# Attention with the head values as stationary operand, the sums left with columns on partitions, and the second network's output projection mixed into its attention

## Chip, cores and metric

The kernel runs on one core of a Trainium2 chip. The metric is the device time of one execution in microseconds; the kernel before was timed three times, and the median counts. A profiled execution gives the trace; its span runs from the first instruction to the last.

## What is computed

Two networks of two layers each run one after the other on 256 tokens of width 1024, in float32. A layer of the first network has three branches (retention, a chunked attention with 8 heads of 64, and a differential attention), gates and merges them, multiplies by `w_out`, and follows with a feed-forward network. A layer of the second has a feed-forward network, then a mixer of three parts whose outputs are laid side by side (256 columns of a short convolution, 256 of a gated MLP, 512 of an attention with 8 query heads on 2 key/value heads), its output projection, and a second feed-forward network. The parts that the change touches, cut to the core:

```python
# first network, chunk attention: s are scores with a relative bias
p = jax.nn.softmax(s, axis=-1).astype(v.dtype)
o = jnp.einsum('bhqk,bkhd->bqhd', p, v)

# second network, short convolution
z = c_gate * h                       # then a causal convolution of width 3 per column: y
return b_gate * y

# second network, attention: three branches that share the queries
pc = masked_softmax(sc, cmp_end[None, :] <= t[:, None])      # 15 compressed keys
o_cmp = jnp.einsum("bgrsn,bngd->bsgrd", pc.astype(vc.dtype), vc)
...
o = g[..., 0, None] * o_cmp + g[..., 1, None] * o_s + g[..., 2, None] * o_w

mix = jnp.concatenate([y_a, y_b, y_c], axis=-1) @ w_out[l]
x = layer_norm(ALPHA * x + mix, ln2_g[l], ln2_b[l])
```

With 256 tokens the selected and the windowed branch both see all earlier keys, so each is a causal attention with keys and values of its own.

## The kernel before

A Python planner (`Plan`, `script`) writes one list of steps, and each engine's function then runs through the whole list and issues what it has to do for each step, in that order. Every engine works its own part strictly in this order and waits on semaphores for operands and free buffers.

**Weights.** A weight matrix comes in units of 1 MB (`P.unit`): SyncE loads a unit into one of three `raw` buffers, ScalarE rounds it to the high part (`high`, L1655), VectorE forms the low part (`low`, L1895), both into one of three `hl` buffers. A product of float32 precision is three rounded matmuls (`mm3`, L200 to L203: high by high, high by low, low by high), so a unit gives 48 matmuls of 256 columns or 24 of 512. Activations are kept as high and low parts too: `XT`, `O1`, `O2`, all with columns on partitions and tokens along the free axis. The step `need` that stands ahead of a unit's matmuls puts the load, the `high` and the `low` of the unit two further on into the list, in one piece.

**Attention.** The 256 queries are two blocks i = 0, 1 of 128, with K = 128(i+1) keys. A task is a block and four heads (two pairs j, each with a lower and an upper half hh of the partitions). `score_pair` (L1491) makes scores for four heads into two PSUM banks; `soft` takes the row maximum on VectorE (L2015) and the exponential on ScalarE (L1741), whose sums go to `rs`. `weigh` turns the unscaled weights in blocks of 128x128 on TensorE (L1372) and copies them to `et`, in turns by ScalarE (L1749) and VectorE (L2022). `values` (L1514) then multiplies, per head and key block, with `et` (128x128) as stationary and the head's values (128x64) as moving operand, so that queries stand on partitions:

```python
for n, (o, vs) in enumerate(outs):
    for mt, v in enumerate(vs):
        x = n * len(vs) + mt
        ins = e.matmul(o, et.ap[:, x * 128:(x + 1) * 128], v, start=mt == 0, stop=mt == len(vs) - 1)
```

In the first network `ca_norm` divides by the sums (L2045), and `turn_split` turns the result back with four transposes for each block and splits it into high and low for the projection. In the second, `nsa_collect` (L2255 to L2268) weights and adds the three branches of a block in `YC`, and `finish` turns and splits them. The compressed branch makes its values for all 8 heads (`cmp_out`, L1572, 512 columns), masks its scores (`cmp_mask`), turns them (`cmp_turn`, L1627) and multiplies (`cmp_values`, L1633). These matmuls (L1491, L1514, L1552, L1572, L1633) take float32 operands without the split, and the trace shows two matmul instructions for each of them. `cmp_hidden` (L1552) is of this kind too; its outputs lie on partitions 0 to 29 and 32 to 61 by turns, from stationary operands of 30 columns.

**Order.** `slots` runs the tasks staggered: in slot n the scores of task n, the values of n-2, the transposes of n-1. `mix(a, b, share)` lays attention steps between pieces of projection units by costs written out by hand (`PART` = 1.44 for a quarter of a unit). In the second network `SHARE2` = 1.4 mixes the attention with the last input projections; when these are used up, the attention goes on alone until all weights are turned (the mark "turned"), and what is left of it is mixed with the output projection at 0.45. The convolution (`conv`: one product, six tap steps and a last product on VectorE, then its split, L2178 to L2190 and L1809) is one step behind the last input projection. `residual` (L1453) puts the scaled input into the accumulators, `out_part` multiplies the first half of `w_out_2` (convolution and MLP rows), `out_end` the attention's half.

## Time and profile before

| what | value |
| --- | --- |
| median of 3 executions | 2088.54 us (2085.18 to 2094.77) |
| profiled execution, its own time | 2087.4 us |
| its span | 2085.4 us |
| TensorE matmul busy | 2046.5 us, 98% of the span |
| VectorE busy | 1241.1 us, 60% |
| ScalarE busy | 926.4 us, 44% |
| weights and other data read | 349.43 MB, 168 GB/s over the span |

In the profile PE is TensorE's matmul, PEld its weight load, DVE is VectorE, ACT ScalarE, POOL GpSimd, SP SyncE. A matmul's time in the trace runs from its start to its modelled end, and matmuls overlap, so the pace of a series is read from starts, and from the chain of waits, where each step is given only the time that it adds. The granted clock (PEclk) is a share of the full TensorE clock.

### The profile page before, as it was taken

What the parts mean: (1) busy time and instruction counts of PE and PEld (TensorE: products, weight loads), DVE (VectorE), ACT (ScalarE), POOL (GpSimd) and SP (SyncE); (2) the same over time, 40 slices, a digit from 0 to 9 for tenths busy, and PEclk for the clock granted to TensorE, in tenths of its full rate; (3) what the DMA queues carried; (4) which work ended last, traced back from release to release, by engine and by line L of the source; (5) the groups of instructions that cost most, each with busy time, mean ns of one, the idle gap of its engine ahead of it and who ended that gap; (6) DMA issues with size and microseconds to landing.
All of it is one profiled execution on the core that took longest, in us unless ns stands there. A gap on an engine that the chain in (4) does not pass through costs nothing.

```text
span 2085.4 us, 32609 instructions
## 1 busy us (share of the span) xinstructions
PE 2046.5 (98%) x14392; PEld 1877.9 (90%) x14392; DVE 1241.1 (60%) x1554; ACT 926.4 (44%) x1278; POOL 44.2 (2%) x56
## 2 busy tenths in 40 slices
PE   7999999999999999999999999899999999989998
PEld 6889999999888999999999988799999998879997
DVE  5555656555655565655665566565566556656555
ACT  3444544443544444444444444344444445434442
POOL 0000000000000000000000001000000000100000
PEclk9999999999999999999999999999999999999999
DMA  7544455766554455586666654258656665435663
GB/s 268 176 131 142 159 185 154 216 184 194 168 162 142 142 163 182 157 242 186 175 182 182 191 146 130 81 144 253 182 166 197 183 182 146 139 98 165 183 182 101
DMA packets 415893, 352.59 MB, mean 169 GB/s; under 512 B 28704, under 2 KB 360840, under 8 KB 415624
## 3 DMA queue, kind: packets, MB, share of 16 engines
q1 hardware_dynamic: 415752, 350.51, 56.0%
q8 instruction: 113, 1.85, 0.4%
q14 instruction: 28, 0.23, 0.0%
HBM read 349.43 MB, written 1.05 MB: 168 GB/s over the span
## 4 chain that ended last, share of the span: by engine, by line
PE 94%; DVE 3%; ACT 2%; DMA 1%; POOL 0%; issue 0%; DVEq 0%; SPq 0%
PE ps L201 28%; PE ps L202 28%; PE ps L203 28%; PE ps L1372 3%; PE ps L1514 2%; PE ps L1453 1%; PE ps L1491 1%; DVE hl L1895 1%; DMA raw<-in_w_in 1%; PE ps L1494 1%; ACT hl L1655 1%; DVE xt L1972 0%; ACT tm L1697 0%; PE ps L1552 0%; ACT er L1741 0%; PE ps L1496 0%
## 5 line engine op out<-in xcount | busy, mean ns | idle before, releaser
L1895 DVE TENSOR_TENSOR hl<-raw,hl 128x2048 fp32r<-128x2048 f32 (+2 forms) x333 | 738.6, 2222 | 466.8 <-ACT hl L1655 466.8
L201 PE MATMUL ps<-xt,hl 128*128 128x256 f32 (+1 forms) x2672 | 755.7, 283 | 0.0
L202 PE MATMUL ps<-xt,hl 128*128 128x256 f32 (+1 forms) x2672 | 746.2, 279 | 0.0
L203 PE MATMUL ps<-xt,hl 128*128 128x256 f32 (+1 forms) x2672 | 745.8, 279 | 0.0
L1655 ACT ACTIVATE hl<-raw 128x2048 fp32r<-128x2048 f32 x324 | 614.9, 1900 | 209.5 <-PE ps L203 192.1
L201 PEld LDWEIGHTS ps<-xt,hl 128*128 128x128 f32 (+1 forms) x2672 | 501.4, 188 | 4.8 <-issue 1.7
L202 PEld LDWEIGHTS ps<-xt,hl 128*128 128x128 f32 (+1 forms) x2672 | 501.2, 188 | 4.4 <-issue 1.2
L203 PEld LDWEIGHTS ps<-xt,hl 128*128 128x128 f32 (+1 forms) x2672 | 501.0, 188 | 0.2
L201 PE MATMUL ps<-hl,o 128*128 128x512 f32 x656 | 261.7, 399 | 0.0
L203 PE MATMUL ps<-hl,o 128*128 128x512 f32 x656 | 259.4, 395 | 0.0
L202 PE MATMUL ps<-hl,o 128*128 128x512 f32 x656 | 259.4, 395 | 0.0
L201 PE MATMUL ps<-hl,xt 128*128 128x512 f32 (+1 forms) x576 | 209.7, 364 | 7.2 <-DVE hl L1895 4.8
L202 PE MATMUL ps<-hl,xt 128*128 128x512 f32 (+1 forms) x576 | 202.8, 352 | 0.0
L203 PE MATMUL ps<-hl,xt 128*128 128x512 f32 (+1 forms) x576 | 202.6, 352 | 0.0
L1725 ACT ACTIVATE th<-ps 128x256 f32<-128x256 f32 x132 | 50.8, 385 | 330.9 <-PE ps L203 330.9
L203 PEld LDWEIGHTS ps<-hl,o 128*128 128x128 f32 x656 | 123.2, 188 | 29.8
L201 PEld LDWEIGHTS ps<-hl,o 128*128 128x128 f32 x656 | 123.2, 188 | 26.9 <-issue 0.5
L202 PEld LDWEIGHTS ps<-hl,o 128*128 128x128 f32 x656 | 123.3, 188 | 26.8 <-issue 0.5
L201 PEld LDWEIGHTS ps<-hl,xt 128*128 128x128 f32 x576 | 109.0, 189 | 25.6 <-DVE xt L1972 6.2
L203 PEld LDWEIGHTS ps<-hl,xt 128*128 128x128 f32 x576 | 108.8, 189 | 16.1
L202 PEld LDWEIGHTS ps<-hl,xt 128*128 128x128 f32 x576 | 109.0, 189 | 14.0
L1999 DVE SCALAR_TENSOR_TENSOR tm<-th,ps 128x256 f32<-128x256 f32 x132 | 55.5, 420 | 103.6 <-ACT th L1725 96.2
(200 smaller groups left out, 1677.3 us busy)
## 6 DMA issues: line engine op xcount, KB each, us to landing
raw<-in_w_in SPq DMA_DIRECT2D x84, 1024.0 KB, 5.1
raw<-in_w_ffn_in SPq DMA_DIRECT2D x88, 512.0 KB, 5.2
raw<-in_ffn_gate SPq DMA_DIRECT2D x88, 512.0 KB, 4.0
raw<-in_ffn_up SPq DMA_DIRECT2D x88, 512.0 KB, 5.3
raw<-in_ffn_down SPq DMA_DIRECT2D x44, 1024.0 KB, 5.1
raw<-in_w_ffn_out SPq DMA_DIRECT2D x22, 1024.0 KB, 5.3
raw<-in_w_out SPq DMA_DIRECT2D x16, 1024.0 KB, 5.1
raw<-in_w_branch_a SPq DMA_DIRECT2D x8, 1024.0 KB, 5.2
```

The source lines that it names most:

```text
L201: e.matmul(out, l[0], r[0], start=start, stop=False)
L202: e.matmul(out, l[0], r[1], start=False, stop=False)
L203: return e.matmul(out, l[1], r[0], start=False, stop=stop)
L1372: ins = e.transpose(b.ap[:, k * 128:(k + 1) * 128], x, ident)
L1453: ins = e.matmul(b.ap[:, k * 128:(k + 1) * 128], XT[:, z, 4 * c + k, i * 128:(i + 1) * 128], ai, start=first and k == 0 and z == 0, stop=n ...
L1491: e.matmul(b.ap[:, n * K:(n + 1) * K], qs[n][hh], ks[n][hh], start=n == 0, stop=False)
L1494: ins = e.matmul(b.ap[:, n * K + c:n * K + c + 128], l, r, start=False, stop=x == len(bias[hh]) - 1)
L1514: ins = e.matmul(o, et.ap[:, x * 128:(x + 1) * 128], v, start=mt == 0, stop=mt == len(vs) - 1)
L1655: e.activation(m["hl"][:, k % NHL, 0, 0:n], m["raw"][:, k % NRAW, 0:n], ACT.Copy).then_inc(s.high.up(("high", k)), 1)
L1725: e.activation(tha, ga, ACT.Tanh, scale=0.5).then_inc(done.up(th.full), 1)
L1895: e.tensor_tensor(lo[:, c], m["raw"][:, k % NRAW, 0:n][:, c], hi[:, c].bitcast(F), ALU.subtract).then_inc(s.low.up(("low", k), *([("low", ...
L1999: e.scalar_tensor_tensor(tma, tha, 1.0, ga, ALU.add, ALU.mult).then_inc(done.up(th.free), 1)
```

## The change

The constants `own` (now by key/value head) and the new `head` mask serve the compressed branch. The diff, cut:

```diff
-SHARE2 = 1.4
+SHARE2 = 0.95
...
+    def spread(self, g, piece):
+        if piece == 1:
+            self.add("need_high", g + self.ahead)
+        elif piece in (2, 3):
+            self.add("need_low", piece - 2)
...
     def n_parts(w, r, c0, src, src_events, banks, first, last, after=()):
-        g = P.unit(segs, n)
+        g = P.unit(segs, n, True)
         for i in range(2):
             for k0 in (0, 2):
                 add("n_part", ...)
+                P.spread(g, 2 * i + k0 // 2)
...
+    def out_part(w, acc, src_events, c, r=0, ks=(0, 2)):
+        segs, n = wk(w, r * 128, 4, c * 512, 512)
+        g = P.unit(segs, n, True)
+        for n, k0 in enumerate(ks):
+            for i in range(2):
...
+    def out_end(w, acc, src_events, o1_read, r=4, heads=False):
+        def rows(c):
+            if not heads:
+                return wk(w, r * 128, 4, c * 512, 512)
+            return [(lambda a, g=g: a[64 * g:64 * g + 64, 0:UNIT].rearrange("p (k c) -> p k c", k=4),
+                     w[512 + g * 256:768 + g * 256, c * 512:(c + 1) * 512].rearrange("(k p) c -> p k c", p=64)) for g in range(2)], UNIT
...
-    def slots(tasks):
+    def slots(tasks, order):
         for n in range(len(tasks) + 2):
-            for x in (n, n - 2, n - 1):
+            for x in order:          # (-1, 0, -2, -1) for these two attentions
...
+    def turned(ers, i):              # transposes and copies of weights already scaled
...
# second network's task, after score_pair
+                gate = gts[:, 24 * i:24 * i + 24].rearrange("p (g j b) -> p g j b", g=2, j=4)[:, :, 2 * jp:2 * jp + 2, bno]
+                add("scale", ers, rs, rc, (("gates", l), gate), 128 * T)
+                ets = turned(ers, i)
+                outs = [(hh, lambda ob, hh=hh: ob.ap[64 * hh:64 * hh + 64, jp * 256:(jp + 1) * 256].rearrange("p (n q) -> p n q", n=2),
+                         VS[:, mt, (bno - 1) * 128 + hh * 64:(bno - 1) * 128 + (hh + 1) * 64],
+                         ets[hh].ap[:, 0:2 * T * 128].rearrange("p (n t q) -> p n t q", n=2, t=T)[:, :, mt, :]) for mt in range(T) for hh in range(2)]
+                part(i, "values_t", ets, outs, [("v nsa", l)], [("win read", l)])
...
-        mix(chain(lin_v(), lin_q(1), lin_conv()), steps, SHARE2, False)
-        while "turned" not in at:
-            next(steps)
-        P.flush()
...
-        mix(lin_out(), steps, 0.45)
+        mix(chain(lin_v(), lin_q(1), lin_conv(), beside(chain(lin_conv2(), lin_out()), conv)), steps, SHARE2)
...
# TensorE
+    def values_t(ob, ets, outs, first, last, v_events, after):
+        for n, (hh, o, v, p) in enumerate(outs):
+            ins = e.matmul(o(ob) if callable(o) else o, v, p, start=first and n < 2, stop=last and n >= len(outs) - 2)
...
# VectorE
+    def scale(ers, rs, rc, gate, K):
+        e.reciprocal(rc, rs).then_inc(done.up(), 1)
+        if gate is not None:
+            e.tensor_tensor(r, r, gate[1], ALU.mult).then_inc(done.up(), 1)
+        for hh, er in enumerate(ers):
+            ev = er.ap[:, 0:2 * K].rearrange("p (n k) -> p n k", n=2)
+            e.tensor_tensor(ev, ev, bc(rc[:, 2 * hh:2 * hh + 2], 2, K), ALU.mult).then_inc(done.up(("scaled", er.n)), 1)
```

In words:

- The weights are divided by their sums (and multiplied by the gate) on VectorE before they are turned (`scale`). `values_t` then has the head's values, 128x64, as stationary and the turned weights as moving operand: 128 columns at a time in the first network, 256 (two heads of one key/value head) in the second. Lower and upper halves of the output partitions come by turns, first `hh` = 0, then 1. The sum stands with columns on partitions, so `ca_norm`, `nsa_collect`, `YC` and the transposes behind them go; `o_split` splits it straight from PSUM. All five sums of a block in the second network (four tasks, one compressed branch) gather in one bank.
- The compressed branch makes its values for 2 heads instead of 8 (128 columns instead of 512), scales in `cmp_mask`, spreads its turned weights by the `head` mask on VectorE, and multiplies twice by 256 columns.
- `w_out_2`'s rows of the attention are loaded in another order, as two halves of 64 partitions.
- In `n_parts`, `t_parts`, `lin_v` and `out_part` the load and `high` of a later unit now stand behind the second quarter of a unit, and `low` comes in two halves behind the third and the fourth.
- The convolution is cut into five steps that are laid beside the last input projection unit and the output projection, which itself is mixed into the attention (one `mix` at 0.95 for all).

Two places of the second network's first layer show the new order. On TensorE, the end of the attention: L1372 are the transposes of the weights `er`, L1453 the residual, L1620 the compressed scores, L1627 their transpose, L1514 the values, L201 the first matmul of each triple of the output projection (its triples go on where lines are left out). Before:

```order
L1372 MATMUL ps<-cst,er 128x128 x8
L1620 MATMUL ps<-small,q 128x15 x8
L1514 MATMUL ps<-v,et 128x64 x8
L1372 MATMUL ps<-cst,er 128x128 x8
L1453 MATMUL ps<-ai,xt 128x128 x8
L1627 MATMUL ps<-cst,er 120x128
L1514 MATMUL ps<-v,et 128x64 x8
L1453 MATMUL ps<-ai,xt 128x128 x8
L201 MATMUL ps<-hl,o 128x512
```

Now (L1408 transposes, L1489 residual, L1667 compressed scores, L1561 `values_t`, L1674 and L1683 the compressed branch, L202 to L204 the triples):

```order
L1408 MATMUL ps<-cst,er 128x128 x8
L1489 MATMUL ps<-ai,xt 128x128 x8
L202 MATMUL ps<-hl,o 128x512
...
L1667 MATMUL ps<-small,q 128x15 x8
L1561 MATMUL ps<-et,v 64x256 x4
L202 MATMUL ps<-hl,o 128x512
...
L1408 MATMUL ps<-cst,er 128x128 x8
L202 MATMUL ps<-hl,o 128x512
...
L1561 MATMUL ps<-et,v 64x256 x4
L1674 MATMUL ps<-cst,er 120x128
L1489 MATMUL ps<-ai,xt 128x128 x8
```

Two triples stand where lines are left out first, two after `values_t`, and four after the last transposes; before, no triple stood between the first row and the last.

On VectorE, the same part of the attention, with the convolution (L2178 to L2188 before, its split L1907). Before:

```order
L2015 TENSOR_REDUCE small<-ps 128x2 x2
L2178 TENSOR_TENSOR zb<-th,ps 128x2x256
L2183 TENSOR_SCALAR tm<-zb,small 128x256
L2186 SCALAR_TENSOR_TENSOR tm<-zb,small,tm 128x256 x2
L2183 TENSOR_SCALAR tm<-zb,small 128x256
L2186 SCALAR_TENSOR_TENSOR tm<-zb,small,tm 128x256 x2
L2188 TENSOR_TENSOR tm<-tm,ps 128x512
L1907 SCALAR_TENSOR_TENSOR o<-tm,o 128x512
L2022 COPY et<-ps 128x512
```

Now, from the scaling of one task (L2089 to L2098) over the next task's maximum (L2061) and one tap step of the convolution to the next scaling:

```order
L2098 TENSOR_TENSOR er<-er,small 128x512 x2
L2061 TENSOR_REDUCE small<-ps 128x2 x2
L2237 TENSOR_SCALAR tm<-zb,small 128x256
L2240 SCALAR_TENSOR_TENSOR tm<-zb,small,tm 128x256 x2
L1941 TENSOR_TENSOR hl<-raw,hl 128x1024
L1953 SCALAR_TENSOR_TENSOR o<-ps,o 128x4x128
...
L2068 COPY et<-ps 128x512
L2089 RECIPROCAL small<-small 128x4
L2094 TENSOR_TENSOR small<-small 128x4
```

The copies to `et` no longer stand behind the whole convolution, and low parts of weights come as halves between small steps; the scaling, which waits for the exponentials of its task, now stands ahead of the next task's maximum.

## Rows read from the trace of the kernel before

**Rows 1.** Busy time, share of the span and instructions of each engine (page, part 1)

```profile
PE 2046.5 (98%) x14392; PEld 1877.9 (90%) x14392; DVE 1241.1 (60%) x1554; ACT 926.4 (44%) x1278; POOL 44.2 (2%) x56
```

**Rows 2.** What TensorE waited for: us in total, times, longest

```profile
PE ps L1514 <- ACT et L1749: 7.0, 2, 3.5
PE ps L1627 <- DVE er L2246: 4.6, 2, 2.3
PE ps L1491 <- DVE o L1907: 3.2, 2, 1.6
PE ps L1491 <- ACT q L1677: 1.4, 2, 0.7
```

**Rows 3.** Busy time of each engine by stretch, then granted clock, DMA share, GB/s

```profile
1260.00:1345.00 85.00, 76.87 (x599) 69.36 (x599) 50.03 (x100) 33.22 (x92) 1.30 (x1) 0.94 0.30 95
1783.00:1868.00 85.00, 76.87 (x607) 69.78 (x606) 50.59 (x100) 33.23 (x92) 1.90 (x1) 0.96 0.32 98
130.00:230.00 100.00, 100.00 (x711) 89.38 (x710) 57.53 (x78) 45.76 (x92) 0.00 (x0) 1.00 0.44 144
```

**Rows 4.** Chain of waits, 1328 to 1337 us: start, us that the step adds

```profile
1328.37 0.70 DVE tm L2188
1329.09 0.63 ACT o L1809
1329.72 0.49 ACT et L1749
1330.26 3.68 PE ps L1514 x16
...
1336.94 1.73 PE ps L1514 x16
```

**Rows 5.** TensorE in order of time: start, us to the modelled end, line

```profile
1778.26 0.28 PE L203 MATMUL ps<-xt,hl 128*128 128x256 f32 x1
1778.46 3.69 PE L1552 MATMUL ps<-qkv,gb 128*30 128x128 f32 x64
1782.08 0.39 PE L201 MATMUL ps<-xt,hl 128*128 128x256 f32 x1
1782.30 0.28 PE L202 MATMUL ps<-xt,hl 128*128 128x256 f32 x1
```

**Rows 6.** The same view, two score groups of the first network, each between its neighbours

```profile
132.68 0.71 PE L1491 MATMUL ps<-k,q 64*128 64x128 f32 x8
133.32 0.82 PE L1494 MATMUL ps<-cst,gb 128*128 128x128 f32 x5
...
146.36 1.14 PE L1491 MATMUL ps<-k,q 64*128 64x256 f32 x8
147.42 0.71 PE L1494 MATMUL ps<-cst,gb 128*128 128x128 f32 x4
```

**Rows 7.** Groups of TensorE instructions: count, busy us, mean ns

```profile
L1514 PEld LDWEIGHTS ps<-v,et 128*128 128x128 f32 x288 | 37.7, 207 | 7.6 <-ACT et L1749 7.2
L1552 PEld LDWEIGHTS ps<-qkv,gb 128*30 128x30 f32 x128 | 6.8, 108 | 0.3
L1572 PE MATMUL ps<-w,tm 128*120 128x512 f32 x4 | 3.2, 888 | 0.0
```

**Rows 8.** Groups of VectorE and ScalarE instructions: count, busy us, mean ns

```profile
L2255 DVE RECIPROCAL small<-small 128x8 f32<-128x8 f32 x12 | 2.3, 195 | 0.0
L2268 DVE TENSOR_TENSOR sg<-sg,tm 128x512 f32<-128x512 f32 x8 | 5.5, 692 | 0.3
L2213 DVE TENSOR_TENSOR sg<-sg,gn 128x256 f32<-128x256 f32 x4 | 1.7, 425 | 0.1
L2015 DVE TENSOR_REDUCE small<-ps 128x2 f32<-128x512 f32 x32 | 20.6, 685 | 8.7 <-PE ps L1496 8.7
L1741 ACT ACTIVATE er<-ps,small 128x256 f32<-128x256 f32 x64 | 29.4, 472 | 49.9 <-DVE small L2015 49.9
L1895 DVE TENSOR_TENSOR hl<-raw,hl 128x2048 fp32r<-128x2048 f32 x313 | 716.1, 2291 | 466.8 <-ACT hl L1655 466.8
```

More of the change, by code:

```diff
@@ L311, in C, with unit @@
         return self.m["const"][:, CO[name][0]:CO[name][1]]
-    def unit(self, segs, n):
+    def unit(self, segs, n, spread=False):
         g = len(self.units)
         self.units.append((segs, n))
-        self.add("need", g + self.ahead)
-        return g
+        if not spread:
+            self.add("need", g + self.ahead)
+        return g
+    def spread(self, g, piece):
[3 more added lines that the diff above has]
+            self.add("need_low", piece - 2)
     def prep_next(self):
@@ L338, in settled @@
     def settled(self):
-        out, k, low = [], 0, {}
+        out, k, low, due = [], 0, {}, []
         def begin():
@@ L348, in settled @@
         for kind, args in self.steps:
+            if kind == "need_low":
+                for u in due:
+                    out.append(("low", (u, self.units[u][1], args[0], 2)))
+                if args[0]:
+                    due.clear()
+                continue
+            if kind == "need_high":
+                assert not due
+                while k < min(len(self.units), args[0]):
+                    due.append(begin())
+                continue
+            assert not due or kind not in ("need", "prep")
             if kind == "need":
@@ L561, in out_end @@
             P.ahead = NHL - c
-            us.append(P.unit(*wk(w, r * 128, 4, c * 512, 512)))
+            us.append(P.unit(*rows(c)))
         def part(c, i, ks):
@@ L913, in turn @@
                 TM.give(tm)
-            yield from slots([task(i, jp) for i in range(2) for jp in range(2)])
+            yield from slots([task(i, jp) for i in range(2) for jp in range(2)], (0, -2, -1))
             yield 0.5
@@ L1120, in nsa, with part @@
         def nsa():
-            rss = [(P.small(24), P.small(24)) for _ in range(2)]
-            def collect(i, bno, ob, events, first_):
-                tm = None if first_ else TM.take()
-                add("nsa_collect", l, i, bno, ob, rss[i], gts, YC[i], tm, events, first_)
-                PB.give(ob)
-                if tm:
-                    TM.give(tm)
+            obs, sums = {}, [0, 0]
+            def part(i, kind, *args):
+                if not sums[i]:
+                    obs[i] = PB.take()
+                ob = obs[i]
+                add(kind, ob, *args[:2], sums[i] == 0, sums[i] == 4, *args[2:])
+                sums[i] += 1
+                if sums[i] == 5:
+                    add("o_split", ob, range(4), (), (), [O1[:, z, 4:8, i * 128:(i + 1) * 128] for z in (0, 1)], [o1_before], [("o1 nsa", l, i)], 1.0 / ALPHA)
+                    PB.give(ob)
             def compressed(i):
-                rs, rc = rss[i]
-                er = ER.take()
-                mx = P.small(8)
+                er, mx, rs = ER.take(), P.small(8), P.small(8)
                 bs = [PB.take() for _ in range(2)]
@@ L1145, in compressed @@
                 yield 0.3
-                ob = PB.take()
-                add("cmp_values", l, ob, et)
+                part(i, "cmp_values", l, et)
                 ET.give(et)
                 yield 1.0
-                collect(i, 0, ob, [("cmp sums", l, i)], False)
-                yield 0.2
             def task(i, bno, jp):
-                rs, rc = rss[i]
-                js = (2 * jp, 2 * jp + 1)
-                hs = [[hh * 4 + j for j in js] for hh in range(2)]
+                js, T = (2 * jp, 2 * jp + 1), i + 1
+                rs, rc = P.small(4), P.small(4)
                 def K(hh, j):
@@ L1193, in nsa @@
+            main = slots([task(i, bno, jp) for jp in range(2) for i in range(2) for bno in (1, 2)], (-1, 0, -2, -1))
+            side = chain(lambda: early, at.until("q"), lambda: compressed(0), at.until("conv"), lambda: compressed(1))
             for cost in main:
@@ L1515, in values @@
         ins.then_inc(done.up(ob.full, et.free, *after), 1)
+    def values_t(ob, ets, outs, first, last, v_events, after):
+        if first:
+            e.wait_ge(*T[ob.before])
+        for et in ets:
+            e.wait_ge(*T[et.full])
+        for x in v_events:
+            e.wait_ge(*T[x])
+        for n, (hh, o, v, p) in enumerate(outs):
+            ins = e.matmul(o(ob) if callable(o) else o, v, p, start=first and n < 2, stop=last and n >= len(outs) - 2)
+        ins.then_inc(done.up(ob.full, *(et.free for et in ets), *after), 1)
     def ret_scores(l, h, b, q, k, dh, er):
@@ L2270, in vector_engine, with cmp_turn @@
-    run(steps, dict(start=start, masks=masks, low=low, turn_split=turn_split, rotate=rotate, silu_gate=silu_gate, ln_stats=ln_stats,
+        e.tensor_tensor(ev, ev, bc(rs, 2, 15), ALU.mult).then_inc(done.up(er.full), 1)
+    def cmp_turn(l, i, er, tb, et):
+        e.wait_ge(*T[tb.full])
+        e.wait_ge(*T[et.before])
+        e.tensor_tensor(et.ap[0:120, :].rearrange("p (j q) -> p j q", j=4), bc(tb.ap[0:120, 0:128], 1, 4), bc(C("head")[0:120, :], 2, 128),
+                        ALU.mult).then_inc(done.up(et.full, tb.free), 1)
```

310 lines of the change are left out of this document (149 added, 161 removed).

## The prediction

> **What bounds the kernel now.** First the page: TensorE's matmuls are busy for 98% of the span, VectorE for 60%, ScalarE for 44% [rows 1]. So whatever helps must take work or waits from TensorE, and the other two may take on work where they have room. Then the waits of TensorE [rows 2]: 7.0, 4.6, 3.2 and 1.4 us, each made of two occurrences, one for each layer of the second network. Then the stretches [rows 3]: in the two attention stages of the second network, 85 us each, matmuls are busy for 76.9 us, so 8.1 us are idle in each, and the granted clock is 0.94 and 0.96. In the first network's attention stage it is busy for all of 100 us at full clock. The chain of waits [rows 4] shows the longest wait: the convolution's last product on VectorE, its split on ScalarE (0.63), only then the copy to `et` that stood behind it in ScalarE's queue, then the values: 16 instructions in 3.68 us, where the same 16 take 1.73 a little later. The first pace is that of the half clock (1.2 of 2.4 GHz) and follows 3.5 us of idleness.
>
> **The change, part by part.**
>
> *Values.* Now 288 matmul instructions [rows 7] at 1.73/16 = 0.108 us [rows 4] make 31.1 us. The 128 columns of stationary `et` cost the same as before however few columns move. With `values_t` each product still gives two instructions, but lower and upper halves of the output partitions come by turns and may run side by side. No row shows this with 64 stationary columns. The nearest is `cmp_hidden`, whose outputs also lie in two column groups: 64 instructions take 1782.08 - 1778.46 = 3.62 us [rows 5], so 0.113 a pair for 128 moving columns. For 256 columns I add what the score groups show, four pairs in 1.06 instead of 0.64 us [rows 6], 0.105 a pair: 0.218. Going into such a group and out again costs something: from the start of L203 to that of the second plain matmul behind are 4.04 us [rows 5], less 0.24 for two plain steps and 3.62 for the pairs, 0.18. Short groups lose more: four pairs in 0.64 us are 0.19 above 4 x 0.113 [rows 6]. Between 0.18 and 0.37 I take 0.3. The first network has 48 pairs of 128 columns in 8 groups (4 pairs for a task of the first block, 8 for the second), the second network 48 pairs of 256 columns in 16 groups (2 and 4). That is 24 x 0.3 + 48 x 0.113 + 48 x 0.218 = 7.2 + 5.4 + 10.5 = 23.1 us, **8.0 less**. With 0.18 a group it is 20.2, 10.9 less.
>
> The trace's 108 ns for a load of 30 columns against 207 for 128 [rows 7] matter here: in rows 5 the loads are hidden, and 64 columns lie between. The Trainium skill, "TensorE: Matmul & The Clock Gate", section "Part 3: Packing small matmuls — row/col tiling", says that a weight load overlaps with a running matmul only when its row group differs, and two column groups on all 128 rows don't differ in it. The rows speak against it for 30 columns, since 64 loads of 108 ns would not fit into 3.62 us beside their matmuls; what it would do for 64 is a rival below.
>
> *Transposes behind the values.* 8 for each of four layers go, 32 at 0.108 (the pace of such an instruction [rows 4], an estimate): **3.5 less**. Those of the weights stay.
>
> *Compressed branch.* L1572 moves 128 columns instead of 512; its four instructions are busy for 3.2 us [rows 7]. A quarter would save 2.4, but the first layer's two ran at low clock, which is counted below: **1.3 less**. The last product has as many columns as before, in two parts: nothing.
>
> *Waits of the second network's attention.* They are bounded by rows 3: 2 x 8.1 idle, and 0.06 x 85 + 0.04 x 85 = 8.5 lost in clock, 24.8 us at most; none at least, if each wait is only replaced. Each of the named causes is addressed: the convolution is cut up and no longer stands ahead of the `et` copies, a bank or a transpose waits behind half a `low` (about 1.15 us) instead of 2.3 [rows 8], and triples of the output projection stand between transposes and values where there were none. Between the scores of the last task and its transposes now stand some 9 us of TensorE work, against a chain for it of 2 x 0.685 (maximum), 4 x 0.472 (exponentials) [rows 8] and the scaling, 0.195 + about 0.2 + 2 x 0.692 = 1.8: 5.1 us. The 1.4 us for the copy of the queries stay, since scores follow it as closely as before; I leave 3.6 for new ones. **19.8 less**, nearer to the upper bound, since the chain is shorter than its cover.
>
> *VectorE.* Scaling adds, for each layer of the second network, 8 x 0.37 + 8 x 0.425 + 8 x 0.692 = 11.9 us; `nsa_collect` took 6 x 0.37 + 10 x 0.692 = 9.1 [rows 8]. So its 50.3 us [rows 3] become 53, in a stage of about 85 - 16 = 69 us: 77%. That fits, but scaling waits for the exponentials, and behind it in the queue stand the next maximum and the next `low`; who waits for these is TensorE, one and two units later. In the first network scaling (4 x 0.2 + 4 x 0.425 + 4 x 0.692, 5.3 us a layer) takes the place of `ca_norm` where VectorE is busy for 57.5 of 100 us [rows 3]: nothing; without that room TensorE would wait for each scaling, 1.8 us.
>
> *Units spread, loads moved.* `high` stands a quarter of a unit later and `low` up to three quarters; both are due two units later. VectorE already idles 466.8 us ahead of `low` [rows 8], which covers the second start for each unit. SyncE's next load waits for `low`, so it starts about half a unit later; the DMA share of 0.30 [rows 3] and three buffers cover it, and the two halves of 64 partitions for `w_out_2` too. If that cover went, `high` would wait for data and TensorE for `low`.
>
> **Sum.** 8.0 + 3.5 + 1.3 + 19.8 = 32.6 us from the profiled execution's 2087.4: 2054.8. That execution lies 1.1 below the median of 2088.5, so against the median I say **2056 us**. With the best ends (10.9 + 3.5 + 2.4 + 24.8) it is 2047; with half of the waits left, 2064.
>
> **Rivals.**
> 1. *Loads of 64 columns aren't hidden.* (207 - 108)/98 = 1.0 ns a column [rows 7], 34 columns more than in rows 5, two loads to a pair: 0.07 us x 96 pairs = 6.5 us, 2062. For it: no row has 64 columns in this form. Against: rows 5. The skill's rule above would give at least this.
> 2. *The halves don't run side by side.* Then a pair costs twice as much, 0.226 and 0.436, together 15.8 more: 2072. For it: the two groups write one bank. Against: `cmp_hidden` writes one bank too [rows 5].
> 3. *The waits only move.* Five sums gather in one bank for each block while the output accumulators are taken, so that few banks go round for scores and transposes; a bank wait is in rows 2 already (3.2 us). If only 5 of the 24.8 us go: 2071.
> 4. *Rivals 2 and 3 together:* 2087, no change.
> 5. *Slower: scaling at the head of VectorE's queue.* It waits for exponentials; the next maximum and `low` wait behind it; the next exponentials wait for that maximum. If this closes to a loop, a task of the second block costs 1.4 + 1.9 + 1.8 + 2.3 (`low`) and 1.9 for `high` on ScalarE, 9.3 us in series, where TensorE has 69/8 = 8.6 us of work. It decides from about 1.5 us a task: with 2 us for each of 16 tasks, 32 us come on top of the 19.8 that stay away, 2108 with the clock still full. Against: `low` and maximum are short beside the distances in the new order.
>
> **How the numbers follow.** Chances: forecast 0.62, rival 1 0.08, rival 2 0.08, rival 3 0.14, rival 4 0.04, rival 5 0.04. The forecast alone spans 2047 to 2064. Down from 2056, 2045 adds a little for the spread of the runs; up, 2073 takes in rivals 1, 2 and 3, and leaves out 4 and 5 and the tails. A measurement of this kernel can tell about 0.5%, 10.4 us: faster means under 2078. Forecast and rivals 1 to 3 lie there, 0.92, of which I take off 0.01 for the upper tail of rival 3: faster 0.91, same 0.05, slower 0.04.
>
> **What would show it.** In the profile after: `values_t` of 256 columns starting in pairs, four pairs in about 0.9 us; no transposes of `sg` or `tm` ahead of the projections except those of the gated MLP and the differential attention; TensorE's waits for ACT et and DVE er gone, those for the queries' copy left; each attention stage at least 9 us shorter than before with a granted clock of 0.98 or more; VectorE busy for over 70% of it. A granted clock under 0.95 there, or waits of TensorE for VectorE of over 8 us in sum, would make the part on waits wrong; single starts, 0.21 apart, that on the values; any new wait outside the second network's attention, that on the units.

## The result and the profile after

The change takes 2058.12 us (median of 4 runs, 2057.47 to 2059.94), the kernel before 2087.85 us beside it: ratio 0.9858, 95% interval 0.9838 to 0.9877. The prediction said 2056 us, faster. The gain of 1.4% is small, but clear of the spread of the runs. The profiled execution has a span of 2055.5 us, 29.9 less than before's 2085.4.

The page's first part, which answers to [rows 1], gives VectorE 62% of the span instead of 60%, and TensorE's matmuls 99%:

```profile
PE 2027.4 (99%) x14272; PEld 1847.5 (90%) x14272; DVE 1268.7 (62%) x1845; ACT 925.8 (45%) x1274; POOL 40.4 (2%) x56
```

What TensorE waits for (us in total, times, longest; against [rows 2]). The four old waits are gone. In their place stand 1.6 and 0.7 us for scaled weights and factors in the second network, and the first line, which is new: nine waits for a half of `low`. Two of them stand at the start of the kernel, the longest, 4.8, which before had too, and one of 0.7. The other seven, 3.4 us together, stand behind layer norms: six in the feed-forward stages and one in the first network's second attention. The second network's attention stages have none.

```profile
PE ps L202 <- DVE hl L1941: 8.9, 9, 4.8
...
PE ps L202 <- DVE xt L2018: 2.3, 9, 0.3
PE ps L1674 <- DVE er L2311: 1.6, 2, 0.8
...
PE ps L1561 <- DVE small L2089: 0.7, 2, 0.4
```

Busy time by stretch, the columns of [rows 3]: the two attention stretches of 85 us are now 69, the clock is 1.00 in both, and VectorE is busy for 79% of them. In the first network TensorE still has no idle time.

```profile
1260.00:1329.00 69.00, 67.82 (x547) 57.32 (x546) 54.38 (x125) 32.55 (x91) 0.00 (x0) 1.00 0.36 100
1768.00:1837.00 69.00, 67.83 (x550) 57.42 (x548) 54.33 (x125) 33.28 (x91) 0.00 (x0) 1.00 0.36 100
130.00:230.00 100.00, 100.00 (x721) 87.67 (x720) 61.34 (x103) 48.68 (x100) 0.00 (x0) 1.00 0.43 143
```

**Stages.** To see where time went, a sharp mark is wanted that both kernels have. The turn of a layer norm's output on TensorE is one. Before, ahead of and behind the second network's first attention (in order of time: start, us, line):

```profile
1231.01 1.09 PE L1372 MATMUL ps<-cst,xs 128*128 128x128 f32 x8 [0.31 <-ACT xs L1688]
...
1361.74 1.03 PE L1372 MATMUL ps<-cst,xs 128*128 128x128 f32 x8
```

After:

```profile
1230.10 1.09 PE L1408 MATMUL ps<-cst,xs 128*128 128x128 f32 x8 [0.30 <-ACT xs L1739]
...
1344.58 1.03 PE L1408 MATMUL ps<-cst,xs 128*128 128x128 f32 x8
```

So this stage went from 130.7 to 114.5 us. Read in the same way, all stages and all runs (us; "first" is the start of the kernel to the first residual and holds the first network's first attention, "FFN" is the first network's first feed-forward stage, one of six that differ alike; a single run has one number for its time):

| kernel | time | first | first network, layer 1, attention | FFN | second network, attention 0 / 1 |
| --- | --- | --- | --- | --- | --- |
| before | 2087.85 | 306.8 | 308.0 | 181.8 | 130.7 / 129.3 |
| the change | 2058.12 | 305.2 | 306.5 | 182.5 | 114.5 / 114.5 |
| low halves unit by unit | 2051.67 | 304.5 | 305.5 | 181.8 | 114.5 / 114.5 |
| units in one piece | 2067.94 | 304.4 | 305.7 | 181.8 | 124.0 / 121.0 |
| old mixing (two mixes) | 2061.42 | 305.2 | 306.5 | 182.5 | 116.4 / 116.4 |
| convolution whole | 2062.18 | 305.2 | 306.5 | 182.5 | 116.8 / 116.8 |
| mixing and convolution undone | 2064.68 | 305.0 | 306.5 | 182.5 | 118.9 / 117.4 |
| all three undone | 2080.41 | 303.9 | 305.7 | 181.8 | 129.0 / 129.2 |
| one half of the partitions first | 2059.04 | 305.5 | 307.5 | 182.5 | 114.5 / 114.5 |
| scaling left out | 2055.21 | 304.9 | 306.6 | 182.5 | 113.4 / 113.4 |
| low unit by unit, share 0.8 | 2056.38 | 304.7 | 305.5 | 181.8 | 117.6 / 116.0 |
| low unit by unit, share 1.1 | 2065.30 | 305.0 | 305.5 | 181.8 | 120.5 / 121.7 |

A stage that an edit doesn't touch comes back within 0.1 us in these profiles, the first one, with the start of the kernel, within 0.5, so differences of 1 us in a stage are readable from single runs, though one of the whole time hardly is.

**Values.** TensorE in order of time, a group of 8 pairs (128 columns, first network) and one of 4 pairs (256 columns):

```profile
182.82 0.28 PE L204 MATMUL ps<-xt,hl 128*128 128x256 f32 x1
183.03 1.09 PE L1561 MATMUL ps<-et,v 128*64 128x128 f32 x16
184.05 0.39 PE L202 MATMUL ps<-xt,hl 128*128 128x256 f32 x1
184.28 0.28 PE L203 MATMUL ps<-xt,hl 128*128 128x256 f32 x1
...
1292.19 0.27 PE L204 MATMUL ps<-xt,hl 128*128 128x256 f32 x1
1292.39 1.08 PE L1561 MATMUL ps<-et,v 128*64 128x256 f32 x8
1293.41 0.38 PE L202 MATMUL ps<-xt,hl 128*128 128x256 f32 x1
1293.63 0.28 PE L203 MATMUL ps<-xt,hl 128*128 128x256 f32 x1
```

Within a group the trace's single starts come in twos, 6 to 7 ns apart, and the twos follow each other by 0.109 us at 128 columns and 0.216 at 256 (the first step is 0.05 longer). From the matmul ahead to the second one behind are 1.46 and 1.44 us; less two plain steps (0.24) and the pairs (0.87 and 0.86), 0.35 and 0.34 are the price of a group's borders. The loads are hidden at this pace (groups: count, busy us, mean ns):

```profile
L1561 PE MATMUL ps<-et,v 128*64 128x256 f32 x96 | 13.9, 395 | 0.7 <-DVE small L2089 0.7
L1561 PE MATMUL ps<-et,v 128*64 128x128 f32 x96 | 7.0, 281 | 0.0
L1561 PEld LDWEIGHTS ps<-et,v 128*64 128x64 f32 x192 | 10.7, 136 | 6.2 <-issue 3.0
```

Two loads of 136 ns go with each pair, and a pair takes 109. The Trainium skill, "TensorE: Matmul & The Clock Gate", section "Part 3: Packing small matmuls — row/col tiling", has loads overlap with a running matmul only where the row group differs. All these use 128 rows, so the rows above disagree, now for 64 columns too.

**The new wait.** Behind a layer norm two units are begun at once, and their halves of `low` are put in this order: first half of unit 1, first half of unit 2, second half of unit 1, second half of unit 2. VectorE and TensorE around 351 us in the change:

```profile
349.30 1.23 DVE L1941 TENSOR_TENSOR hl<-raw,hl 128x1024 fp32r<-128x1024 f32 x1 [0.93 <-ACT hl L1706]
351.10 3.50 DVE L1941 TENSOR_TENSOR hl<-raw,hl 128x1024 fp32r<-128x1024 f32 x3 [0.58 <-ACT hl L1706]
...
353.51 0.38 PE L202 MATMUL ps<-xt,hl 128*128 128x256 f32 x1 [0.43 <-DVE hl L1941]
```

VectorE does one half, then stands still for 0.58 us until ScalarE has made the second unit's high part, though the first unit's second half could be done at once. That half comes third of the four and ends, two halves behind 351.10, at 353.46, and TensorE starts at 353.51. The profile counts the wait, 0.43 us, only from the modelled end of the matmul ahead; the stage as a whole is 0.7 us longer than before. Before, two whole units ran unit by unit:

```profile
350.83 4.49 DVE L1895 TENSOR_TENSOR hl<-raw,hl 128x2048 fp32r<-128x2048 f32 x2 [0.93 <-ACT hl L1655]
```

### The profile page after: what moved, and what is told of

Read it like the earlier page. It is cut to its first block, busy times and chain, and to the rows that moved or that the text cites. A ratio compares the mean times of both kernels' runs of the same rounds, so it can differ in the third digit from the quotient of the medians.

```text
span 2055.5 us, 32684 instructions
## 1 busy us (share of the span) xinstructions
PE 2027.4 (99%) x14272; PEld 1847.5 (90%) x14272; DVE 1268.7 (62%) x1845; ACT 925.8 (45%) x1274; POOL 40.4 (2%) x56
## 4 chain that ended last, share of the span: by engine, by line
PE 92%; DVE 4%; ACT 2%; DMA 1%; SPq 0%; issue 0%; POOL 0%; DVEq 0%
PE ps L202 28%; PE ps L203 28%; PE ps L204 28%; PE ps L1408 2%; DVE hl L1941 2%; PE ps L1489 1%; ACT hl L1706 1%; PE ps L1527 1%; DMA raw<-in_w_in 1%; PE ps L1561 1%; PE ps L1530 1%; ACT tm L1748 0%; DVE xt L2018 0%; PE ps L1599 0%; PE ps L1532 0%; PE ps L1550 0%
## 5 line engine op out<-in xcount | busy, mean ns | idle before, releaser
L1941 DVE TENSOR_TENSOR hl<-raw,hl 128x1024 fp32r<-128x1024 f32 (+2 forms) x572 | 757.5, 1356 | 407.4 <-ACT hl L1706 407.2
L202 PE MATMUL ps<-xt,hl 128*128 128x256 f32 (+1 forms) x2672 | 754.8, 282 | 2.6 <-DVE hl L1941 2.6
L204 PE MATMUL ps<-xt,hl 128*128 128x256 f32 (+1 forms) x2672 | 745.5, 279 | 0.0
L202 PEld LDWEIGHTS ps<-xt,hl 128*128 128x128 f32 (+1 forms) x2672 | 501.0, 187 | 10.3 <-DVE hl L1941 4.0
L204 PEld LDWEIGHTS ps<-xt,hl 128*128 128x128 f32 (+1 forms) x2672 | 500.7, 187 | 0.2
L202 PE MATMUL ps<-hl,o 128*128 128x512 f32 x656 | 261.6, 399 | 0.0
L204 PE MATMUL ps<-hl,o 128*128 128x512 f32 x656 | 259.4, 395 | 0.0
L202 PE MATMUL ps<-hl,xt 128*128 128x512 f32 (+1 forms) x576 | 210.4, 365 | 8.7 <-DVE hl L1941 6.3
L204 PE MATMUL ps<-hl,xt 128*128 128x512 f32 (+1 forms) x576 | 203.0, 352 | 0.0
L204 PEld LDWEIGHTS ps<-hl,o 128*128 128x128 f32 x656 | 123.2, 188 | 29.8
L202 PEld LDWEIGHTS ps<-hl,o 128*128 128x128 f32 x656 | 123.2, 188 | 27.5 <-issue 0.8
L202 PEld LDWEIGHTS ps<-hl,xt 128*128 128x128 f32 x576 | 109.1, 189 | 28.2 <-DVE hl L1941 7.4
L204 PEld LDWEIGHTS ps<-hl,xt 128*128 128x128 f32 x576 | 109.0, 189 | 16.2
```

The lines of the kernel that those rows point to most:

```text
L202: e.matmul(out, l[0], r[0], start=start, stop=False)
L204: return e.matmul(out, l[1], r[0], start=False, stop=stop)
L1941: e.tensor_tensor(lo[:, c], m["raw"][:, k % NRAW, 0:n][:, c], hi[:, c].bitcast(F), ALU.subtract).then_inc(s.low.up(("low", k), *([("low", ...
```

## Experiments

The questions were: does the new wait come from the order of halves, which of the three rearrangements (spread units, mixing, convolution) carried the waits of the second network's attention, is the side by side of `values_t` what it seems, and what does scaling cost.

**Low halves unit by unit**

```diff
-                for u in due:
-                    out.append(("low", (u, self.units[u][1], args[0], 2)))
+                mine = due if len(due) < 2 else due[args[0]:args[0] + 1]
+                for u in mine:
+                    for h in ((0, 1) if len(due) > 1 else (args[0],)):
+                        out.append(("low", (u, self.units[u][1], h, 2)))
```

> The change kept whole; only where two weight units are due at once (after each layer norm) are the low halves put unit by unit: both halves of the first unit behind the third quarter, both of the second behind the fourth, so that the first unit is complete before VectorE turns to the second. Theory A (the order of the halves causes the new waits): in the trace of the change each of nine places behind a layer norm has TensorE wait 0.4 to 0.9 us for the last half of the first unit, 8.9 us in sum for nine waits; they go, each later feed-forward stage is back at its length before (181.9 instead of 182.5), and the whole takes about 2054, 4 us less than the 2058.1 of the change. Theory B (ScalarE's second high is late, in whatever order the halves stand): the waits move to the second unit's halves and the time stays at 2058.

Measured: 2051.67 us (5 runs, 2051.54 to 2052.07), ratio to before 0.9833 (0.982 to 0.9846), span 2049.6. The waits for `low` fall to the two at the start of the kernel, which the expectation had counted among its nine places behind a layer norm; VectorE now does four halves in a row, and the first unit is complete after the first two:

```profile
PE ps L202 <- DVE hl L1943: 5.8, 2, 4.8
```

```profile
348.56 4.63 DVE L1943 TENSOR_TENSOR hl<-raw,hl 128x1024 fp32r<-128x1024 f32 x4 [0.93 <-ACT hl L1708]
```

Theory A holds, with more than expected: 0.7 us in each of the six feed-forward stages, 4.1 together, 1.0 in the first network's second attention and 0.7 ahead of the first residual; 5.9 by the spans. The last of these is hardly more than that stage's own spread (304.5 to 305.0 in the four runs with this order of halves, 305.0 to 305.2 in five that have this stage as the change has it), and no wait in the profile's list that went explains it.

**Units in one piece**

```diff
-        if not spread:
-            self.add("need", g + self.ahead)
+        self.add("need", g + self.ahead)
...
     def spread(self, g, piece):
+        if piece >= 0:
+            return
```

> The change with its units in one piece again: load, high and both low halves of a later unit stand ahead of a unit's matmuls, as before, also in the attention stages; all else is the change's. Theory A (spreading is a price in the feed-forward stages and a gain in the attention): the six later feed-forward stages are 0.6 us shorter each, 4 in sum, and the two attention stages of the second network (114.5 us each from layer norm to layer norm) are longer, since a bank or a transpose waits behind a whole low of 2.3 us instead of 1.15: 1 to 4 us each, VectorE's waits behind them in TensorE's list. Together 2056 to 2062. Theory B (spreading did nothing for the attention, its waits went through the other parts): attention stages at 114.5, the whole at 2054.

Measured: 2067.94 us (2067.69 to 2068.57). The feed-forward stages are as expected, but the attention stages of the second network lose 9.5 and 6.5 us, not 1 to 4. TensorE waits for VectorE at several places, for the factors of the scaled weights, for a copy to `et` and in the compressed branch:

```profile
PE ps L1562 <- DVE small L2090: 4.0, 4, 1.1
PE ps L1562 <- DVE et L2069: 3.8, 2, 1.9
PE ps L1675 <- DVE small L2090: 3.4, 2, 2.5
```

Part of the loss is clock, as the columns of [rows 3] show for these two stages:

```profile
1231.00:1350.00 119.00, 113.63 (x842) 97.25 (x842) 79.60 (x158) 51.96 (x111) 6.22 (x5) 0.96 0.48 124
1748.00:1864.00 116.00, 109.09 (x843) 93.83 (x842) 79.55 (x158) 51.89 (x111) 6.22 (x5) 1.00 0.53 137
```

TensorE is idle for 5.4 and 6.9 us, in the change for 1.2 in each, and in the first of the two the clock is 0.96, by estimate 0.04 x 119 = 4.8 us. So waits grow by 4.2 and 5.7 us, and the larger loss of the first layer is the clock's.

Theory A, with its size wrong: spreading the units is the largest single part of the change. The edit undoes two things at once, the later place of load and `high` and the cutting of `low`; no run separates them.

**Old mixing of attention and output projection**

```diff
-        mix(chain(lin_v(), lin_q(1), lin_conv(), beside(chain(lin_conv2(), lin_out()), conv)), steps, SHARE2)
+        mix(chain(lin_v(), lin_q(1), lin_conv(), beside(lin_conv2(), conv)), steps, 1.4, False)
+        mix(lin_out(), steps, 0.45)
```

> The change with its order at the second network's attention undone: attention steps mixed with the last input projections at a share of 1.4, and only what is left then mixed with the output projection at 0.45; convolution in steps, halves of units, scaling and values_t stay. Theory A (the weight work between the last scores, transposes and values hid the chain through VectorE and ScalarE): TensorE waits again for the scaled weights or the copies to et, each attention stage is 4 to 8 us longer (118 to 122 us from layer norm to layer norm) and its granted clock falls under 0.98; the whole at 2066 to 2074. Theory B (the waits went because the convolution and the whole low no longer stand ahead of the copies): stages within 1 us of 114.5, the whole at 2057 to 2060.

The edit brings back the two mixes and their shares. The order of the tasks and of the steps within a slot, and the place of the second compressed branch, stay those of the change; no run undoes them.

Measured: 2061.42 us, stages 1.9 us longer, at a clock of 1.00. That lies between the theories: waits come back, but small ones, and the 1.4 us for the queries' copy, absent in the change, are among them:

```profile
PE ps L1675 <- DVE er L2312: 3.0, 4, 1.2
...
PE ps L1562 <- ACT small L1847: 2.0, 2, 1.0
PE ps L1528 <- ACT q L1729: 1.4, 2, 0.7
```

**Convolution in one piece**

```diff
         def conv():
             hs, bcg = comp["conv"]
+            for _ in range(3):
+                yield
             add("conv_gate", l, bcg, hs)
...
-            yield
             yt = TM.take()
             for c in range(2):
                 add("conv_taps", l, c, yt, cols, cols_event)
-                yield
...
-            yield
             add("conv_split", l, yt, [O1[:, z, 0:2, :] for z in (0, 1)], o1_before)
```

> The change with the convolution in one piece again (product, six taps, last product and split together, put at the fourth of its five places); everything else is the change's. Theory A (the convolution as a block ahead of scaling and copies made the wait of the chain in rows 4): TensorE waits again about 3 us for a copy or a scaled weight in each layer, stages 117 to 119 us instead of 114.5, the whole at 2063 to 2067. Theory B (with projection work between scores, transposes and values the block is covered): stages within 0.5 us of 114.5, the whole at 2058.

Measured: 2062.18 us, stages 2.3 us longer. That is close to theory A's size, but its cause is another. There is one wait a layer: the first triple of the output projection waits for the convolution's split (L1952 is the low part of an output operand), and no copy or scaled weight is late.

```profile
PE ps L202 <- DVE o L1952: 4.1, 2, 2.1
```

**All three undone**

> Three parts of the change undone together: units in one piece, the old order of attention and output projection, the convolution in one piece. What is left of the change is scaling ahead of the transposes, values_t, the missing transposes behind it, the small compressed branch and the spread mask. Alone, one piece made the two attention stages 9.6 and 6.5 us longer, the old order 1.9 each. Theory A (the parts cover for each other, each alone hides what another would leave): together they cost more than the sum of the single ones, 14 to 20 us a stage, stages of 128 to 134 us, and the whole is at 2078 to 2090, so that the values alone bring nothing because their scaling adds to the waits. Theory B (they add): stages of 126 and 123 us, what the values and transposes save by count (4.3 us a layer) is kept, and the whole is at 2072 to 2076.

The edit is those of the last three together; the order of the tasks stays the change's here too. Measured: 2080.41 us, stages of 129.0 and 129.2. Singly the three cost 9.5 + 1.9 + 2.3 = 13.7 and 6.5 + 1.9 + 2.3 = 10.7, together 14.5 and 14.7: near theory B's sum in the first layer, theory A's 14 to 20 in both, and a whole time as theory A has it. Part of this is clock again, 0.97 and 0.96. The longest wait behind the start of the kernel is 5.2 us, in each layer, for the weights of the second compressed branch:

```profile
PE ps L1675 <- DVE er L2312: 13.7, 4, 5.2
PE ps L1562 <- DVE small L2090: 6.7, 4, 2.9
```

The chain of waits shows how it is made (start, us that the step adds):

```profile
1324.16 0.70 DVE tm L2246
...
1325.42 1.91 ACT hl L1707
...
1327.35 2.29 DVE hl L1942
1329.64 0.20 DVE small L2297
...
1331.47 0.30 DVE er L2312
...
1331.81 0.47 PE ps L1675
```

The convolution's last product (L2246) releases its split on ScalarE, behind which the next unit's `high` (L1707) stands; VectorE waits for that, makes a whole `low` (L1942), and only then goes on with the compressed weights (L2297 to L2312), for which TensorE waits. A unit's high and low part, 1.91 + 2.29 us, stand in series in the middle of an attention chain.

**Mixing and convolution undone, units spread**

> Old order of attention and output projection and the convolution in one piece, as in the run with three parts undone, but with the units spread in quarters and low in halves. Theory A (spreading is what carries the waits of the second network's attention): stages near 114.5 + 1.9 + 2.3 = 118.7 us, so 10.4 less than the 129.1 with one piece, the whole at 2066 to 2068. Theory B (the parts cover for each other, spreading needs the new order): stages of 122 us or more, the whole above 2072.

Measured: 2064.68 us, stages of 118.9 and 117.4 against 118.7 expected. The same chain, from the same product (L2245 here) on, goes straight through, with no `high` or `low` in it, and TensorE's longest wait for these weights is 2.2 instead of 5.2 us:

```profile
1322.68 0.70 DVE tm L2245
...
1323.40 0.64 ACT o L1860
...
1324.07 0.69 DVE o L1953
1324.76 0.27 DVE er L2290 x2
...
1326.97 0.29 DVE er L2311
...
1327.31 0.32 PE ps L1674
```

```profile
PE ps L1674 <- DVE er L2311: 5.0, 4, 2.2
```

Theory A: spreading alone, with the old mixing, is worth 10.1 and 11.8 us a stage. TensorE's idle time falls from 12.2 to 4.2 us in each (windows of 124 us, and of 114 and 112), and the clock goes from 0.97 and 0.96 to 0.99 and 1.00. No part of `low` stands in this stretch of the chain at all, so the place of the weight work may count for as much as its cutting.

**One half of the output partitions first** (the first network's edit; the second network's is alike)

```diff
-                         ets[hh].ap[:, (n * T + mt) * 128:(n * T + mt + 1) * 128]) for n, j in enumerate(js) for mt in range(T) for hh in range(2)]
+                         ets[hh].ap[:, (n * T + mt) * 128:(n * T + mt + 1) * 128]) for hh in range(2) for n, j in enumerate(js) for mt in range(T)]
```

> The change with the products of values_t in another order: first all of the lower half of the output partitions, then all of the upper half, instead of by turns. Same instructions, same operands. Theory A (the two column groups run side by side only when they come by turns): pairs of 109 ns (128 columns) and 216 ns (256) become single starts of 0.109 and 0.216, 48 x 0.109 + 48 x 0.216 = 15.6 us more TensorE time, less what the stages of the second network take back from their small waits: 2070 to 2074. Theory B (128 rows by 64 columns is quick for another reason): the pace stays and the time is 2058.

Measured: 2059.04 us, only 1 more, so theory A seems to have fallen. The starts tell more. The group that took 1.46 us by turns:

```profile
182.15 0.28 PE L204 MATMUL ps<-xt,hl 128*128 128x256 f32 x1
182.35 1.58 PE L1561 MATMUL ps<-et,v 128*64 128x128 f32 x16
183.87 0.39 PE L202 MATMUL ps<-xt,hl 128*128 128x256 f32 x1
184.09 0.28 PE L203 MATMUL ps<-xt,hl 128*128 128x256 f32 x1
```

takes 1.94 now, 0.49 more in each of the four groups of this size; the two in the first network's second attention are its 1.0 us in the table. In the program its 16 instructions are 8 of the lower half, then 8 of the upper. The single starts are 0, 160, 269, 378, 487, 493, 597, 653, 706, 762, 815, 872, 981, 1090, 1199 and 1308 ns: five alone, 0.109 apart after the first step, then two series interleaved, each at 0.109, then the rest alone. The second series begins 6 ns behind the fifth start, when three of the lower half haven't started; so the ninth instruction is let go ahead of the sixth. (The records don't name the half; this is the reading that fits the two series, which have eight starts each.) Where only four of a half stand before the other half, in all groups of 8, both start together, 13 ns apart instead of 6. So the two halves do run side by side, which halves the price at 128 columns (alone 0.109 an instruction, together 0.109 for two), and TensorE finds the partner up to about four instructions ahead by itself. The price of 256 columns on one half alone was not measured. The section of the Trainium skill named above says that matmuls start strictly in program order; by this reading the trace doesn't agree.

**Scaling left out**

```diff
-            ev = er.ap[:, 0:2 * K].rearrange("p (n k) -> p n k", n=2)
-            e.tensor_tensor(ev, ev, bc(rc[:, 2 * hh:2 * hh + 2], 2, K), ALU.mult).then_inc(done.up(("scaled", er.n)), 1)
+            e.tensor_tensor(er.ap[:, 0:1], er.ap[:, 0:1], rc[:, 2 * hh:2 * hh + 1], ALU.mult).then_inc(done.up(("scaled", er.n)), 1)
```

> The change with the scaling of the weights cut to its first column: reciprocal and gate factor stay, of the two products of 128 x 2K elements for each four heads only a column is left. The kernel so leaves out the division of the weights by their sums and their gate. Theory A (VectorE has room, scaling is hidden): TensorE waits 0.7 us for the factors and 1.6 for the compressed weights in the change; at most these and the pace around them go, the attention stages of the second network stay between 113 and 114.5 us each, the whole at 2055 to 2058. Theory B (scaling is a price in series, at the head of VectorE's queue): 1.1 to 1.4 us for each task of the second block come back, 8 tasks in the second network, 4 in the first: 2041 to 2047.

Measured: 2055.21 us, 2.9 less than the change; the second network's stages 113.4, so 1.1 each, the first network's unchanged within 0.3. Theory A: scaling is hidden but for 1.1 us a layer of the second network. Reciprocals and gate factors stay in this run, so what they cost is not in it.

**Shares of 0.8 and 1.1 with low unit by unit**

> The change with the low halves unit by unit (2051.7) and the second network's mix at a share of 0.8 instead of 0.95, so that more projection work lies between attention steps and attention ends later. Theory A (the order has room left): the two remaining waits, 0.4 for the factors and 0.8 for the compressed weights a layer, go: 2049 to 2051. Theory B (the rest is pace at the borders of groups, not waits): 2051 to 2053, or more if attention is left over at the end.

> The change with the low halves unit by unit (2051.7), the second network's mix at a share of 1.1 instead of 0.95: less projection work between attention steps. At 0.8 each stage had become 3.0 and 1.5 us longer, with waits for the compressed branch at its end. Theory A (0.95 lies at the best place, both sides lose): stages 115 to 117 us instead of 114.5, the whole at 2052.5 to 2057. Theory B (0.8 lost because attention ended too late, so an earlier end gains): stages 113 to 114, the whole at 2049 to 2051.

Measured: 2056.38 and 2065.30 us. Both sides lose. At 0.8 the stages are 3.1 and 1.5 us longer, and the time is above theory B's range, which it allowed for attention left over at the end; TensorE waits 6.2 us for the compressed branch's factors. At 1.1 they are 6.0 and 7.2 us longer, more than theory A said, the largest wait again that for the compressed weights, 2.7 us a layer:

```profile
PE ps L1676 <- DVE er L2313: 5.4, 2, 2.7
```

By these waits attention waits for VectorE where too little weight work stands between its steps. That with too much its end comes late is the likely reading of 0.8, but not shown by itself. 0.95 is the best of the three.

**The change and the low halves unit by unit, again, on one chip**

> The change itself, beside the next run on the same chip: 2058 again, stages of the second network's attention 114.5 us.

> The change with the low halves unit by unit once more, beside the change on the same chip. Theory A (the difference is the order of the halves): 2051.7 again, 6.4 less than the change beside it. Theory B (the difference was between chips or days): within 2 us of it.

Measured: 2057.09 us (2056.56 to 2057.39) and 2051.98 us (2051.53 to 2052.13), so 5.1 between them by the medians and 5.9 by the spans (2055.4 and 2049.5). The version with low halves unit by unit beats both kernels: ratio to before 0.9827 (0.9805 to 0.9849) here, 0.9833 the first time.

## Why the prediction was right, and where it was not

The forecast of 2056 us came true at 2058.12, and its mechanism is in the main the one that the runs show. That it came so near is in part luck: two errors of opposite sign, 5.9 us for the units and 3.5 for the waits, partly cancelled.

- *Values, 8.0 less.* By the measured prices, 24 x 0.35 + 48 x 0.109 + 48 x 0.216 = 24.0 us instead of 23.1: 7.1 less. The pairs together were right to 2%; the border of a group is 0.35 rather than 0.3, near the upper bound that short score groups gave.
- *First network.* Values and transposes there were to bring 2.5 (96 x 0.108 - 8 x 0.3 - 48 x 0.113) and 1.7 us, 4.3 unrounded. With the low halves in good order its two stages are 2.3 and 2.5 us shorter, 4.8; in the change itself 1.5 each. Scaling costs nothing there, as forecast.
- *Second network's attention.* The forecast had 28.3 us: 5.5 for values, 1.7 for transposes, 1.3 for the compressed branch and 19.8 for waits. The stages lost 16.2 + 14.8 = 31.0. Less values at the measured prices (20.7 - 16 x 0.35 - 10.4 = 4.7), and 1.7 and 1.3 taken as forecast, 23.3 us came from waits and clock, against an upper bound of 24.8. Idle time alone fell by 13.9 (8.1 us in each of windows of 126 and 124 us before, 1.2 in the change). The term was right in kind and 3.5 too small. The reckoning given, a chain of 5.1 us against 9 us of cover, rests on the new order; by the runs the spread units carry most of it (10.1 and 11.8 us with the old mixing, 9.5 and 6.5 with the new), the mixing 1.9 and the convolution 2.3 a layer. The prediction had all three, but didn't weigh them.
- *Compressed branch.* The four instructions of its values are busy for 1.0 instead of 3.2 us, as the quarter of the columns should have it (2.4 less forecast, 1.1 of that counted with the clock):

```profile
L1619 PE MATMUL ps<-w,tm 128*120 128x128 f32 x4 | 1.0, 322 | 0.0
```

- *The wait for the queries' copy* was to stay, 1.4 us, "since scores follow it as closely as before". It went, and came back, 1.4 to 1.6 us, in all three runs with the old mixing: a misread of the order.
- *VectorE.* Scaling had no term of its own in the second network, only 3.6 us left for new waits; it costs 1.1 us a layer. VectorE's 79% in the stretch was forecast as 77%. Nearer to the old kernel the gain is almost gone: with all three parts undone the stages are only 1.7 and 0.1 us shorter than before, though values, transposes and compressed branch save (4.7 + 1.7 + 1.3) / 2 = 3.9 a layer. Scaling on VectorE's path, ahead of the transposes, is one possible taker of the rest. The changed order of the tasks, which that run keeps, is another. Neither is shown: no run leaves out scaling there, and none restores the old order of the tasks.
- *Units spread: nothing.* **This step failed.** It said that both parts "are due two units later" and that VectorE's idle 466.8 us cover the later start. That holds in the middle of a stage. It doesn't hold behind a layer norm in seven places, where the next unit is due soon and two are begun together, so that the order of four halves decides. Putting them right gives back 5.9 us of span: 6 x 0.69 in the feed-forward stages, 1.0 in the first network's second attention, and 0.7 in its first stage, where the cause is open. The prediction's own sign for this, "any new wait outside the second network's attention", is the first line of the waits.
- *Rival 1* (loads not hidden) and *rival 2* (halves not side by side) fell by the starts, *rival 3* and *rival 5* (waits only move, scaling closes a loop) by the stretches. Rival 3's picture is nonetheless in part what the units in one piece bring: of the 31.0 us in the two attention stages 15.0 remain.

The sum closes: 4.8 + 31.0 - 5.9 = 29.9, the difference of the spans.

## What to carry to other kernels

A long operation that serves another stream (here 2.3 us of `low` behind 1.9 of `high`) should be cut up and its parts spread where it shares a queue with a short chain for which the bottleneck waits; here that was worth 9.5 and 6.5 us a stage, the other two rearrangements 1.9 and 2.3. When such an operation is cut, look at every place where two of them come due together, here behind the layer norms, and finish the one that is needed first. And work taken off the bottleneck at the price of a longer chain through another engine pays only with enough other work, in small pieces, between the steps: the whole change made a stage 15 to 16 us shorter, with the three rearrangements undone at most 1.7 remained.

## What the hardware showed that was not expected

Matmuls of 64 stationary columns on different halves of the output partitions ran side by side in these traces (two in 0.109 us at 128 columns, two in 0.216 at 256), also when four of one half stood ahead of the other half, and one was let go ahead of three that stood before it in the program, if the two series of starts are read rightly. Loads of 136 ns, two for a pair of 109, cost nothing there, but entering and leaving such a group cost 0.35 us, so long groups are better than short ones.
